# Sample memory attention in native fp32 matmuls, and a new order of the end of the attention stage

## The reference

```
q = qm.reshape(b, t, MEM_HEADS, MEM_HEAD_DIM) * (MEM_HEAD_DIM ** -0.5)
s = jnp.einsum('bthd,bmhd->bhtm', q, k)
p = jax.nn.softmax(s, axis=-1)
return jnp.einsum('bhtm,bmhd->bthd', p, v).reshape(b, t, MEM_WIDTH)
```

## Time and profile before

| | us |
|---|---|
| median of three runs (1003.74 to 1004.60) | 1004.59 |
| the profiled execution | 1005.05 |
| its span, first to last instruction | 1003.10 |
| PE busy (5725 matmuls) | 936.9, 93% |
| DVE busy | 541.3, 54% |
| ACT busy | 445.7, 44% |
| POOL busy | 60.4, 6% |

### The profile page before, as it was taken

One profiled execution on the slowest core, in us unless ns is written; L12 is line 12 of the kernel. 1 busy time (PEld: TensorE's weight loads), 2 busy tenths in 40 slices (PEclk: granted clock), 3 DMA queues, 4 the chain that ended last, 5 costly groups with the idle time before them and its releaser, 6 DMA issues. The chain is left out here.

```text
span 1003.1 us, 15526 instructions
## 1 busy us (share of the span) xinstructions
PE 936.9 (93%) x5725; PEld 845.3 (84%) x5725; DVE 541.3 (54%) x953; ACT 445.7 (44%) x743; POOL 60.4 (6%) x52
## 2 busy tenths in 40 slices
PE   5989999999899999999999999999668699999995
PEld 5967999999799999999999988888657588888884
DVE  3476335322346678787788568666564443133344
ACT  4674211122222567666757445777533433133210
POOL 0020002212100000000000000002312000000000
PEclk9999999999899999999999999999968799999998
DMA  9865432223352677787786633211410734214123
GB/s 361 291 233 161 148 112 84 84 90 102 138 213 87 201 253 242 237 242 252 244 250 199 219 127 137 95 48 41 175 59 1 267 127 157 101 62 140 52 84 105
DMA packets 75050, 155.96 MB, mean 155 GB/s; under 512 B 9096, under 2 KB 43337, under 8 KB 72984
## 3 DMA queue, kind: packets, MB, share of 16 engines
q1 hardware_dynamic: 74032, 148.16, 44.3%
q10 hardware_dynamic: 944, 6.82, 1.8%
HBM read 143.56 MB, written 11.50 MB: 155 GB/s over the span
## 5 line engine op out<-in xcount | busy, mean ns | idle before, releaser
L158 ACT ACTIVATE w_hi<-w_raw 128x1024 fp32r<-128x1024 f32 (+1 forms) x78 | 81.8, 1049 | 245.2 <-PE z_acc L68 138.8
L165 DVE TENSOR_TENSOR w_lo<-w_raw,w_hi 128x1024 fp32r<-128x1024 f32 (+1 forms) x78 | 96.0, 1230 | 173.4 <-ACT w_hi L158 173.3
L66 PE MATMUL z<-x_hi,w_hi 128*128 128x288 f32 x512 | 154.7, 302 | 0.0
L67 PE MATMUL z<-x_lo,w_hi 128*128 128x288 f32 x512 | 151.8, 297 | 0.0
L68 PE MATMUL z<-x_hi,w_lo 128*128 128x288 f32 x512 | 151.8, 296 | 0.0
L66 PE MATMUL z_acc<-x_hi,w_hi 128*128 128x288 f32 x352 | 104.2, 296 | 0.0
L67 PE MATMUL z_acc<-x_lo,w_hi 128*128 128x288 f32 x352 | 103.8, 295 | 0.0
L68 PE MATMUL z_acc<-x_hi,w_lo 128*128 128x288 f32 x352 | 103.5, 294 | 0.0
L66 PEld LDWEIGHTS z<-x_hi,w_hi 128*128 128x128 f32 x512 | 97.2, 190 | 3.4 <-issue 1.1
L67 PEld LDWEIGHTS z<-x_lo,w_hi 128*128 128x128 f32 x512 | 97.2, 190 | 1.3 <-issue 0.2
L68 PEld LDWEIGHTS z<-x_hi,w_lo 128*128 128x128 f32 x512 | 97.0, 190 | 0.0
(11 more groups left out here) (444 smaller groups left out, 2052.5 us busy)
## 6 DMA issues: line engine op xcount, KB each, us to landing
w_raw<-in_w_feat SPq DMA_DIRECT2D x56, 512.0 KB, 4.4
k_raw<-in_cache SPq DMA_DIRECT2D x128, 192.0 KB, 3.1
v_raw<-in_cache SPq DMA_DIRECT2D x128, 128.0 KB, 2.6
o_raw<-in_w_out SPq DMA_DIRECT2D x32, 512.0 KB, 3.9
w_raw<-in_w_mem_kv SPq DMA_DIRECT2D x16, 512.0 KB, 3.5
gate_spill<-gate_tmp SPq DMA_DIRECT2D x16, 288.0 KB, 3.3
mix<-gate_spill SPq DMA_DIRECT2D x4, 1152.0 KB, 10.0
x_nat<-in_x ACTq DMA_DIRECT2D x4, 1024.0 KB, 7.4
```

The costliest lines, as they stand in the source:

```text
L66: pe.matmul(out, a[0], b[0], start=start, stop=False)
L67: pe.matmul(out, a[0], b[1], start=False, stop=False)
L158: act.activation(s.whi[:, u % SPL, 0:w], s.wraw[:, u % RAW, 0:w], ACT.Copy).then_inc(s.w_hi, 1)
L165: dve.tensor_tensor(s.wlo[:, u % RAW, 0:w], s.wraw[:, u % RAW, 0:w], f32(s.whi[:, u % SPL, 0:w]), ALU.subtract).then_inc(s.w_lo, 1)
```

## The change

The sample's scores and values become single native float32 matmuls on the loaded units and on plain `F32` blocks of queries and probabilities. The splitting of the units (`unit_high`, `unit_low`) goes, with its buffers and waits, and so does the splitting of the placed queries and turned probabilities. SP loads five units early instead of three, and reuses a unit's semaphore once PE has used the unit. The banks of the sample's scores and sums change places. The hand-written orders of ACT, DVE and PE are new.

```
-UR = 4
+EARLY = 5
-        p_c, p_d, p_e = p_qk[:, 0, 0:MT], p_s[:, 2, :], p_qk[:, 1, :]
+        p_c, p_d, p_e = p_s[:, 2, 0:MT], p_qk[:, 0, :], p_qk[:, 1, :]
...
                         if g:
-                            sp.wait_ge(u_hi, v + 1)
+                            sp.wait_ge(u_used, v + 1)
...
-                        load_units(0, 3)
+                        load_units(0, EARLY)
                 sp.wait_ge(sc_ps, 4 * NH)
-                load_units(3, 8)
+                load_units(EARLY, 8)
                 sp.wait_ge(o_ps, NH)
                 load_units(8, 16)
-            def unit_high(act, u): ...
-            def unit_low(eng, u): ...
...
                 def g_score(g, b):
+                    u = 8 * g + b
                     if b == 0:
-                        pe.wait_ge(qa_lo, 4 + MH + 1 + MH * g + MH)
-                        pe.wait_ge(ct_lo, 3)
+                        pe.wait_ge(qa_hi, 4 + MH + 1 + MH * g + MH)
                         if g:
                             pe.wait_ge(g_exp, g)
-                    k = unit_split(8 * g + b)
+                        else:
+                            pe.wait_ge(nmax, 4 * NH)
+                    pe.wait_ge(u_in[b], 16 * g + 16)
                     for h in range(MH):
                         i = MH * b + h
-                        last = product(pe, p_c, [t[:, P * i:P * i + P] for t in qp], [t[:, MT * h:MT * h + MT] for t in k], i == 0, i == 15)
+                        last = pe.matmul(p_c, qp[:, P * i:P * i + P], unit(u)[:, MT * h:MT * h + MT], start=i == 0, stop=i == 15)
...
-                    v = unit_split(8 * g + 4 + b)
+                    pe.wait_ge(u_in[4 + b], 16 * g + 16)
                     for m in range(2):
-                        last = product(pe, p_d, ...)
+                        last = pe.matmul(p_d, pp[:, m, P * b:P * b + P], unit(8 * g + 4 + b)[:, MW * m:MW * m + MW],
+                                         start=b == 0 and m == 0, stop=b == 3 and m == 1)
```

More of the change, by code:

```diff
@@ L1285, in attention_stage @@
         vmh, vml = at("vm_hi", [P, 2, MW], F32R), s.memkv_lo
[L1288 to L1295, removed]
+        raws = [at("mu_a", [P, EARLY, 2 * MW]), place(nc, scored, "mu_b", [P, 8 - EARLY, 2 * MW]), place(nc, valued, "mu_c", [P, 8, 2 * MW])]
+        assert at.at <= s.early[1] - 8 * HEAD_W
         at = Map(nc, 0)
-        qp = [at("q_pad_hi", [P, 16 * QROW], F32R), at("q_pad_lo", [P, 16 * QROW], F32R)]
-        pp = [place(nc, s.early[1] - 8 * HEAD_W, "p_pad_hi", [P, 2, 4 * MROW], F32R), at("p_pad_lo", [P, 2, 4 * MROW], F32R)]
+        qp, pp = at("q_pad", [P, 16 * QROW]), at("p_pad", [P, 2, 4 * MROW])
         gp, od = s.gp, s.od
@@ L1429, in _ @@
                 pool.memset(f32(ptl[:, 7 * P:8 * P]), 0.0).then_inc(zeroed, 1)
-                unit_low(pool, 1)
                 pool.wait_ge(qk_ps, 2 * NH)
[L1432 to L1439, removed]
+                pool.memset(qp[:], 0.0).then_inc(q_zero, 1)
+                pool.memset(pp[:], 0.0).then_inc(p_zero, 1)
+                pool.wait_ge(p_zero, 1)
             @block.scalar
@@ L1832, in _ @@
                 turned(LASTH - 1, 1)
+                m_keys()
                 gate(LASTH - 2)
+                turned(LASTH - 1, 2)
                 inverses(LASTH)
[L1835 to L1839, removed]
+                g_maxima(0)
+                g_divide(0)
                 gate(LASTH - 1)
@@ L2101, in _ @@
                 turn(LASTH - 1, 1)
+                g_score(0, 0)
                 turn(LASTH - 1, 2)
+                g_score(0, 1)
+                g_score(0, 2)
+                g_score(0, 3)
                 values(LASTH - 1)
-                m_score(0)
                 turn(LASTH, 0)
                 turn(LASTH, 1)
-                g_score(0, 0)
+                g_turn(0)
+                m_score(0)
                 turn(LASTH, 2)
-                g_score(0, 1)
                 values(LASTH)
-                g_score(0, 2)
-                g_score(0, 3)
+                g_value(0, 0)
                 m_score(1)
                 m_turn(0)
-                g_turn(0)
+                g_value(0, 1)
+                g_value(0, 2)
                 m_value(0)
-                g_value(0, 0)
-                g_value(0, 1)
                 m_score(2)
                 m_turn(1)
-                g_value(0, 2)
+                g_value(0, 3)
+                g_score(1, 0)
                 m_value(1)
-                g_value(0, 3)
                 g_out(0)
-                g_score(1, 0)
+                m_score(3)
+                m_turn(2)
                 g_score(1, 1)
-                m_score(3)
                 g_score(1, 2)
+                m_value(2)
                 g_score(1, 3)
-                m_turn(2)
-                m_value(2)
+                m_turn(3)
                 g_turn(1)
-                m_turn(3)
                 g_value(1, 0)
+                m_value(3)
                 g_value(1, 1)
-                m_value(3)
                 g_value(1, 2)
```

110 lines of the change are left out of this document (28 added, 82 removed).

## The result

The changed kernel takes 975.63 us (median of four runs, 974.98 to 976.63) against 1004.6 for the kernel before (median of four, 1003.74 to 1008.24): a ratio of 0.971 (95% interval 0.9689 to 0.973). It was forecast at 977.3, and the range held it. In a later comparison it took 976.84 (six runs) against 1004.32 (17 runs), 0.9729 (0.9706 to 0.9752).

A forecast was written before the change was run, and what follows sets the result against it. PE's work, idle time and clock in the attention stage bound the kernel: 4.8 us more work, 20.0 less idle, 12.1 less half clock. 1005.05 - 27.3 = 977.75, less 0.46 for the median, gives 977.3 us; range 973 to 989.

The forecast's parts named there:

- the range: Forecast time of the whole kernel: 973 to 989 us, leaving out a chance of 0.16.
- the stretch: Attention stage from first memory-key transpose (698.15) to end of last transposes (779.57): 81.42 us, PE busy 57.83.
- half clock: PE's slowed work after long waits in the attention stage: some 12 us before, none expected after.
- The sum: Attention stage: 4.8 us more work, 20.0 less idle, 12.1 less at half clock; 27.3 earlier, giving 977.3.
- The native matmul: Sample scores and values on PE: 0.213 us per 256-column record, 0.427 per 512-column; sixteen units 27.3, adding 4.8.
- The rival of two passes: Native matmul takes two passes, not four, records running side by side: 16 x 0.85 less, 963.7 us; chance 0.02.
- The walk: New order followed from 698.15: last transposes begin at +53.4, 3.6 us idle left.
- The four waits: PE idle 0.6 us in values(7), 1.3 before g_turn(1), 0.8 before g_value(1,0), 0.85 before the last transposes.
- the turns: m_turn(0) to m_turn(3) on PE; the sample unit in between was said to give slack of 1.3 to 2.6 us.
- The clock: PE at full clock throughout the attention stage, longest idle 1.3 us; over 0.97 expected; native matmuls do not lower it.
- POOL and DVE: Memory-head scalings took 3.27 us beside a POOL subtraction, 1.14 without; no such charge, POOL having no work left.
- Loads and queues costed at nothing: SP's unit loads land before PE wants them: cost nothing; without that cover each late unit costs at most 8 us.

The follow-up runs named there:

- the busy POOL: Changed kernel plus eight unread unit subtractions on POOL, two starting at the end of each memory head's exponentials; 989.54 us, ratio 0.9849.
- one subtraction on POOL: Changed kernel plus one unread unit subtraction on POOL, instead of two, at the end of each memory head's exponentials; 977.66 us, ratio 0.9732.
- late loads: Changed kernel with three units loaded early instead of five (EARLY = 3); 974.88 us, ratio 0.9714.
- the split version in the new order: Kernel before, splitting kept, with the new lists and banks and its unit copies and subtractions put where engines were idle; 983.67 us, ratio 0.9777.
- the one with no subtraction on POOL: Kernel before, splitting kept, with new lists and banks, and all 16 unit subtractions on DVE; 981.83 us, ratio 0.9772.
- the native run with the old order: Changed kernel with the three engine orders of the kernel before, splitting steps taken out; 992.48 us, ratio 0.9872.
- the run with filled waits: Kernel before with 63 unneeded 512-column matmuls filling four long waits of PE; 1000.69 us, ratio 0.9946.

## Why the prediction was right

**What bounds it.** Right: the stretch, and in it idle time and half clock. The sum was 4.8 of work added, 20.0 less idle, 12.1 less half clock, 27.3 in all. Measured in the traces: +5.0, -20.9, -11.1, 27.0.

**The native matmul.** Right: 0.216 us for a record of 256 columns, where 0.213 was taken between 0.11 and 0.43 for want of a row. At 512 columns it is 0.428 for 0.427. The rival of two passes, at half the price, is out. That rival hung on a halved rate that the Trainium skill gives (Perfetto Trace Analysis, section "Engine Utilization"): the trace agrees with it for a record, and shows two records for a matmul.

**The walk.** The last transposes begin 53.7 us after the first, for 53.4. The four waits are where they were put, each 0.15 to 0.3 shorter, 0.9 in all. The busy time is 51.1, where 49.9 were counted up to the start of the last transposes (50.3 with them). Of these 1.2 us, 1.0 are in the work that the change leaves alone (46.1 for 45.1), so they were in the kernel before too, and made its half clock 11.1 instead of 12.1. In good part waits and busy time err by one thing: the tail of 0.17 us behind the last record before a wait counts as busy in the profile, and the walk left it to the wait; for four waits that makes an estimated 0.7. The slack ahead of the turns was walked as 1.0, 2.1, 2.6 and 2.3; the busy POOL measured 1.1, 2.2, 2.5, 2.0. The summary of 1.3 to 2.6 leaves out the first of these, and it is there that one subtraction on POOL already made PE wait. One count is wrong without touching the sum: 12 small subtractions of query and probability blocks are gone from DVE (8 and 4), not 24.

**The clock.** Right for the stretch: 1.00. What the prediction said of idle stretches (four above 3.9 to half, one of 1.18 to full) leaves out what lies between, and even the 1.18 was followed by half clock in two of four traces that have it (last section).

**POOL and DVE.** Right, and more than was claimed: the prediction needed only that POOL has no work left. The Trainium skill, page SBUF — State Buffer, section "SBUF: two separate sides", calls the port between them an exclusive lock and no sharing. The traces agree: 1.14, 3.1 to 3.2 and 5.3 to 5.4 us with none, one and two subtractions of 2.4 us beside the scalings, and each subtraction holds one scaling until it is over.

**Loads and queues costed at nothing.** Right: no wait of PE in the stretch is for a unit, and with late loads the waits are the same.

**What it did not say,** and what my next expectation got wrong: how the gain divides. I took the split version in the new order to be as fast as the changed kernel, by adding up each engine's busy time; it is 9 us of stretch behind. The engines have the room, but the steps of each stand in one order, and every step inserted takes from a slack of 1 to 2.5 us. The 9 us are 8.0 more idle time and 5.9 of half clock, less the 5.0 that its matmuls are cheaper.

**How close it came.** The forecast takes 27.3 us off the median of the kernel before. In the traces 27.0 are gone in the stretch and 0.4 behind it. The medians differ by 29.0 in the first comparison, with four runs of each, and by 27.5 in the later one, with 17 and 6. So the 1.7 us by which the forecast is above the first median are for the most part scatter of those medians, and not the fault of a step of the sum.

## What to carry to other kernels

Where PE waits for heads or tiles whose chains run over in-order engines, price a step that you put on ACT or DVE by the slack of the chain that it stands ahead of, not by the idle share of its engine: 2.1 us of delay ahead of each of four heads cost 1.4 us of stretch, and 4.2 cost 12. Matmuls that are dearer on PE (here by 5 us) can pay when they take such steps away (here the stretch is 9 to 10 us shorter all the same). Work on GpSimd that nobody waits for is not free when it runs beside operations of VectorE like these scalings. And look at the end of such a stage: the last copy before the last transposes can be hidden by a piece of work that is due anyway.

## What the runs showed of the hardware

**After a wait of 2 to 3 us PE's clock may be half or full.** In the front stage, where all kernels here are the same, PE waits 2.4 to 2.5 us for a split weight at about 81 us. In the first trace of the kernel before it came back at half clock (a 512-column record of 0.77 us, and the next ones slow), in that of the changed kernel at full clock (0.47):

```profile
82.18 0.77 PE L66 MATMUL z_acc<-w_hi,mem_hi 128*128 128x512 f32 x1 [2.50 <-DVE w_lo L165]
```

```profile
80.96 0.47 PE L66 MATMUL z_acc<-w_hi,mem_hi 128*128 128x512 f32 x1 [2.48 <-DVE w_lo L165]
```

Of the thirteen traces three come back at half (this one, the run with one POOL subtraction and the one with no subtraction on POOL, 0.76) and ten at full. In the native run with the old order a wait of 2.37 us was followed by half clock and one of 2.20 by full:

```profile
724.04 0.76 PE L66 MATMUL pa_o<-pt_hi,vm_hi 128*128 128x512 f32 x1 [2.37 <-DVE pt_lo L1691]
...
737.82 0.47 PE L66 MATMUL pa_o<-pt_hi,vm_hi 128*128 128x512 f32 x1 [2.20 <-DVE pt_lo L1691]
```

The run with POOL busy even has full clock after a wait of 3.03 and half after one of 2.22. All waits of 3.6 us and more that no filling shortened, four in the stretch in each trace of the kernel before, were followed by half clock. And a wait of 1.18 with one of 0.45 behind it, full clock after it in the earlier trace rows, had half clock after it in the second trace of the kernel before and in the run with filled waits, for some 3 us:

```profile
699.23 0.50 PE L66 MATMUL pa_o<-pt_hi,vp_hi 128*128 128x512 f32 x1 [0.45 <-DVE mix L1700]
...
702.61 0.41 PE L66 MATMUL pa_s<-km_hi,qm_hi 128*128 128x256 f32 x1
```

So a kernel with many waits of this size should have times that scatter, and it has: ten runs of the kernel before lay between 999.8 and 1008.4, ten of the changed kernel between 974.5 and 977.8. Over all runs of the kernel before the mean granted clock goes with the time, from 0.981 at 998.2 us to 0.970 at 1008.8.

**Where the stretch begins moves by 5 us over traces of the same front:** 693.1 to 698.5 in thirteen traces. The matmul after the wait at 81 us begins at 80.5 to 82.4, and why that varies stays open. The rest is for the most part half clock at two places, as the distance from that matmul to the stretch shows:

| mean clock, 80 to 90 us | mean clock, 255 to 285 us | traces | distance, us |
|---|---|---|---|
| 1.00 | 0.94 | 4 | 612.5 to 613.5 |
| 1.00 | 0.89 | 5 | 614.4 to 615.0 |
| 0.83 | 0.89 | 4 | 615.2 to 616.3 |

In the last group are the three traces that came back at half and the run with POOL busy, where the clock falls within 3 us of the wait. The first trace of the kernel before is in it, its second trace and the first of the changed kernel in the middle one. So a difference of a few us between two single traces has to be read stage by stage.
